# Split fp32r products for state and offset, and the pooling matrix folded into the output weights

## The reference, cut to what matters

```python
proj = rms_norm(h, norm_mix_w) @ w_in            # [u | z | xBC | dt]
y_pool = einsum(window_mean(u) - u, pool_w) * pool_scale       # 4 groups, windows 2, 4, 8, 16
x, B, C = silu(causal_conv4(xBC))                # 24 heads of 64 in 4 groups, state 128
# per chunk of 128 tokens and group of 6 heads:
y_diag = ((C B^T) * decay) @ (x * dt)
y_off  = exp(a_cs) * (C @ S)                     # S: the state carried from chunk to chunk
S      = S * chunk_decay + B^T @ (x * dt * decay_to_end)
y = (y_diag + y_off + d_skip * x) * silu(z)
y = y * rsqrt(mean(y * y) + eps) * ssm_norm_w    # mean over the 384 columns of the group
h = h + concat([y_pool, y]) @ w_out
h = h + relu(rms_norm(h, norm_ffn_w) @ w_ff1) ** 2 @ w_ff2
out = rms_norm(h, norm_f_w)[16:]
```

## Time and profile before

| | |
|---|---|
| median of 3 runs | 2752.06 us (2752.05 to 2752.53) |
| the profiled execution, its own time | 2754.46 us |
| its span | 2752.7 us |
| mean granted TensorE clock | 0.997 of full speed |
| TensorE busy | 2710.4 us, 98% of the span |
| VectorE, ScalarE, GpSimd busy | 58%, 45%, 40% |
| DMA | 531 MB, 193 GB/s in the mean |

### The profile page before, as it was taken

One profiled execution on the slowest core, in us unless ns is written; L12 is line 12 of the kernel. 1 busy time (PEld: TensorE's weight loads), 2 busy tenths in 40 slices (PEclk: granted clock), 3 DMA queues, 4 the chain that ended last, 5 costly groups with the idle time before them and its releaser, 6 DMA issues.

```text
span 2752.7 us, 37252 instructions
## 1 busy us (share of the span) xinstructions
PE 2710.4 (98%) x13950; PEld 2234.5 (81%) x13950; DVE 1609.6 (58%) x2221; ACT 1234.6 (45%) x2414; POOL 1093.3 (40%) x798
## 2 busy tenths in 40 slices
PE   8999999999999999999999999999999999999998
PEld 6778778888788887888888888878888888888887
DVE  3589833567425665147763466664445666666666
ACT  2367734556424555145552644555445322222323
POOL 1356641132101322003324587865655435353434
PEclk9999999999999999999999999999999999999999
DMA  9687576645556445565436546674444942333323
GB/s 291 206 272 235 198 273 246 240 161 197 182 200 260 157 148 204 198 233 208 167 144 244 189 157 224 238 265 166 154 141 167 350 153 92 138 122 131 122 92 153
DMA packets 225490, 531.12 MB, mean 193 GB/s; under 512 B 14090, under 2 KB 98062, under 8 KB 215838
## 3 DMA queue, kind: packets, MB, share of 16 engines
q1 hardware_dynamic: 225310, 528.74, 53.6%
HBM read 382.74 MB, written 145.95 MB: 192 GB/s over the span
## 4 chain that ended last, share of the span: by engine, by line
PE 92%; ACT 2%; DVE 2%; DMA 1%; issue 1%; POOL 1%; SPq 0%; DVEq 0%; ACTq 0%; POOLq 0%
PE bank L2007 22%; PE bank L1975 21%; PE bank L1697 19%; PE bank L1741 13%; PE bank L1721 6%; PE bank L1819 2%; PE bank L1812 2%; PE bank L1638 1%; PE bank L1793 1%; PE bank L1800 1%; PE bank L1776 1%; ACT E L1388 1%; DMA w_scr<-w_both 1%; PE bank L1760 1%; PE bank L1930 0%
## 5 line engine op out<-in xcount | busy, mean ns | idle before, releaser
L1697 PE MATMUL bank<-hnT_hi,w_ring 128*128 128x512 f32 x1152 | 374.4, 396 | 1.4 <-DMA w_ring<-w_scr 1.3
L2126 DVE SCALAR_TENSOR_TENSOR acc<-pre,par,acc 128x512 f32<-128x512 f32 x240 | 216.3, 901 | 108.7 <-ACT pre L1250 103.0
L2007 PE MATMUL bank<-w_first,T_hi 128*128 128x512 f32 x896 | 276.0, 389 | 0.3 <-issue 0.3
L1697 PEld LDWEIGHTS bank<-hnT_hi,w_ring 128*128 128x128 f32 x1152 | 216.5, 188 | 46.5 <-ACT pre L1250 1.4
L1975 PE MATMUL bank<-T_hi,w_both 128*128 128x512 f32 x768 | 242.6, 390 | 0.6 <-DMA T_lo<-hn_scr 0.4
L1741 PE MATMUL bank<-w_ring,T_hi 128*128 128x512 f32 x768 | 242.0, 396 | 0.0
L2449 DVE TENSOR_TENSOR acc_th<-bank,acc_th 128x512 f32<-128x512 f32 x224 | 149.9, 686 | 153.5 <-PE bank L2007 153.3
L1003 POOL TENSOR_TENSOR small<-small 128x1 f32<-128x1 f32 (+1 forms) x71 | 17.4, 245 | 546.2 <-ACT yo L1333 340.0
L1697 PE MATMUL bank<-hnT_lo,w_ring 128*128 128x512 f32 x576 | 224.8, 390 | 0.0
L1721 PE MATMUL bank<-w_ring,hnT_hi 128*128 128x384 f32 x768 | 198.4, 339 | 0.0
L2007 PEld LDWEIGHTS bank<-w_first,T_hi 128*128 128x128 f32 x896 | 168.1, 188 | 35.6 <-issue 0.7
(11 more groups left out here) (289 smaller groups left out, 6242.5 us busy)
## 6 DMA issues: line engine op xcount, KB each, us to landing
w_ring<-w_scr SPq DMA_DIRECT2D x312, 512.0 KB, 4.2
T_scr<-stage SPq DMA_DIRECT2D x32, 1792.0 KB, 6.8
w_scr<-w_both SPq DMA_DIRECT2D x104, 512.0 KB, 4.3
pair_raw<-in_w_ff SPq DMA_DIRECT2D x36, 1024.0 KB, 5.5
third<-T_scr SPq DMA_DIRECT2D x28, 1024.0 KB, 4.9
pair_raw<-T_scr SPq DMA_DIRECT2D x28, 1024.0 KB, 4.8
sums<-sums_scr SPq DMA_DIRECT2D x64, 384.0 KB, 4.9
raw<-in_w_in SPq DMA_DIRECT2D x36, 512.0 KB, 6.9
```

Of the source, the lines that this page charges most:

```text
L1697: mm = nc.tensor.matmul(bank[s][:, :], w[:, k, :], t[:, k, :], start=(k == 0 and j == 0), stop=(k == KT - 1 and j == 2))
L2007: mm = nc.tensor.matmul(bank[4 * half + t][:, :], a[:, k, tok], w[:, k, :], start=(SECOND[q % 7] not in GOES_ON and k == 0 and j == 0), st ...
L2126: ins = nc.vector.scalar_tensor_tensor(acc[:, s, 0:TB], pre[:, s, k:k + TB], w, acc[:, s, 0:TB], ALU.mult, ALU.add)
```

## The change

- The offset product C @ S and the state product B^T @ xw are done in three fp32r passes each instead of one fp32 matmul. The operands are split: ScalarE writes the high parts of C, S, xw and B (`c_both`, `s_both`, `xw_both`, `b_both`), GpSimd the low parts of C and S, VectorE those of xw and B. The buffers lie in the space of h, so h is loaded later, in the output projection.
- `slot3` is taken apart in `diagonal` and `state`. TensorE's order in a step is now: unit n1; `y_transposes` of q - 2; `diagonal` of q - 1; `slot1`; `state` of q - 1; unit n2; `y_offset`.
- The pooling matrix and scale are multiplied into the output weights once, in block 0 (`fold`: 8 products; four transposes of `pool_w` before), and so is the norm weight of y (`scale_rows`). The pooled values are split as they are.
- `y_high` and `y_low` are one instruction each; the history of the pooling windows is copied by ScalarE; S is scaled right after its low part is written; `state_add` comes before `taps`(n1).

```diff
@@ tensor
-                def y_offset(b, q, g, c):
-                    state_ready.wait(pe, b, q)
-                    nc.tensor.matmul(bank[7][:, 0:GW], group_tile(g, 1)[:, c * P:(c + 1) * P],
-                                     S[:, g, :], start=True, stop=True).then_inc(yoff_ps.sem, 1)
+                def y_offset(b, q):
+                    s_split_lo.wait(pe, b, q + 1)
+                    for j, (i, o) in enumerate(((0, 0), (0, 1), (1, 0))):
+                        mm = nc.tensor.matmul(bank[7][:, 0:GW], c_both[:, i, :], s_both[:, o, :],
+                                              start=(j == 0), stop=(j == 2))
+                    mm.then_inc(yoff_ps.sem, 1)
...
+                def state(b, q):
+                    xw_split_lo.wait(pe, b, q + 1)
                     yo_ready.wait(pe, b, q + 1)
-                    nc.tensor.matmul(bank[7][:, 0:GW], xb[:, GW:GW + P], xw[:, :],
-                                     start=True, stop=True).then_inc(state_ps.sem, 1)
+                    for j, (i, o) in enumerate(((0, 0), (0, 1), (1, 0))):
+                        mm = nc.tensor.matmul(bank[7][:, 0:GW], b_both[q % 2][:, i, :],
+                                              xw_both[:, o, :], start=(j == 0), stop=(j == 2))
+                    mm.then_inc(state_ps.sem, 1)
...
+                        if q > 1:
+                            y_transposes(b, q - 2)
                         if q:
-                            slot3(b, q - 1)
+                            diagonal(b, q - 1)
                         slot1(b, q, g, c)
+                        if q:
+                            state(b, q - 1)
                         for n in n2:
                             unit(b, n)
-                        y_offset(b, q, g, c)
-                        if q:
-                            y_transposes(b, q - 1)
...
+                    def fold(N):
...
+                        pe.wait_ge(raw_ready[N % RING], 16 * (N // RING + 1 + (N % RING == 0)))
+                        for kk in range(2):
+                            nc.tensor.matmul(bank[kk][:, :], pw[:, out_rows(N) + kk, :],
+                                             raw_half(N, kk), start=True, stop=True
+                                             ).then_inc(c_pe, 1)
...
-                                    nc.tensor.matmul(bank[2 + i % 2][:, :], pw[:, i, :],
-                                                     F[:, i * TB:(i + 1) * TB], start=True,
-                                                     stop=True).then_inc(mix_ps.sem, 1)
+                            if b == 0 and u in (1, 2):
+                                fold(N + 3)
@@ gpsimd, in a step behind ty = xb * d_skip
+                        s_split_hi.wait(pool, b, q + 1)
+                        nc.gpsimd.tensor_tensor(c_both[:, 1, :], group_tile(g, 1)[:, c * P:(c + 1) * P],
+                                                c_both[:, 0, :].bitcast(F32), ALU.subtract)
+                        nc.gpsimd.tensor_tensor(s_both[:, 1, :], S[:, g, :],
+                                                s_both[:, 0, :].bitcast(F32), ALU.subtract
+                                                ).then_inc(s_split_lo.sem, 1)
+                        gains_ready.wait(pool, b, 1)
+                        s_split_lo.wait(pool, b, q + 1)
+                        nc.gpsimd.tensor_tensor(by_head(S[:, g, :]), by_head(S[:, g, :]),
+                                                per_head(cd, c, g), ALU.mult
+                                                ).then_inc(scd_ready.sem, 1)
@@ scalar, in a step
+                        nc.scalar.activation(b_both[q % 2][:, 0, :], bank[4 + q % 2][:, GW:GW + P],
+                                             ACT.Copy)
+                        nc.scalar.activation(xb[:, :], bank[4 + q % 2][:, 0:GW], ACT.Copy
...
                         if q:
                             y_squares(b, q - 1)
+                        yoff_ps.wait(act, b, q)
+                        nc.scalar.activation(c_both[:, 0, :], group_tile(g, 1)[:, c * P:(c + 1) * P],
+                                             ACT.Copy)
+                        state_ready.wait(act, b, q)
+                        nc.scalar.activation(s_both[:, 0, :], S[:, g, :], ACT.Copy
+                                             ).then_inc(s_split_hi.sem, 1)
                         tanh(b, n1)
                         if q:
                             y_norm(b, q - 1)
+                        xw_ready.wait(act, b, q + 1)
+                        nc.scalar.activation(xw_both[:, 0, :], xw[:, :], ACT.Copy
+                                             ).then_inc(xw_split_hi.sem, 1)
@@ vector
+                def xw_low(b, q):
+                    xw_split_hi.wait(dve, b, q + 1)
+                    nc.vector.tensor_tensor(xw_both[:, 1, :], xw[:, :],
+                                            xw_both[:, 0, :].bitcast(F32), ALU.subtract
+                                            ).then_inc(xw_split_lo.sem, 1)
@@ sync
-                        if n == 12:
-                            sp.dma_start(h[:, :, :], x_in[0, b * TB:(b + 1) * TB, :].rearrange(
...
+                            if (d, i) == (0, 4):
+                                yoff_ps.wait(sp, b, STEPS)
+                                state_ps.wait(sp, b, STEPS)
+                                sp.dma_start(h[:, :, :], x_in[0, b * TB:(b + 1) * TB, :].rearrange(
```

More of the change, by code:

```diff
@@ L483, in weights_ready, with out_rows, raw_half, scale_rows @@
                 pe.wait_ge(w_loaded[(N - UNITS) % RING], 32 * ((N - UNITS) // RING + 1))
+        PW_SCALED = 7
+        PW_TURNED = 10
+        FOLDED = [U_OUT + d * 8 + u for d in range(2) for u in range(8) if OUT_ORDER[u] < 2]
+        def out_rows(N):
+            return 2 * OUT_ORDER[(N - U_OUT) % 8]
+        def raw_half(N, kk):
+            return raw[:, N % RING, kk * 512:(kk + 1) * 512]
+        def scale_rows(act, N):
+            if N in FOLDED:
+                f = FOLDED.index(N)
+                for kk in range(2):
+                    act.wait_ge(c_pe, PW_TURNED + 2 * f + kk + 1)
+                    last = nc.scalar.activation(raw_half(N, kk), bank[kk][:, :], ACT.Copy)
+            else:
+                for kk in range(2):
+                    w = W_NSSM + out_rows(N) + kk - 4
+                    last = nc.scalar.activation(raw_half(N, kk), raw_half(N, kk), ACT.Copy,
+                                                scale=par[:, w:w + 1])
+            last.then_inc(c_act, 1)
+            act.wait_ge(c_act, PW_SCALED + N - U_OUT + 1)
         def high_part(act, N):
@@ L1243, in evac @@
                         w3 = par[:, W_CONV + 60 + ct:W_CONV + 61 + ct]
-                        nc.scalar.activation(pre[:, s, 0:3], hist[:, ct, :], ACT.Copy
-                                             ).then_inc(hist_read.sem, 1)
+                        hist_read = steps.mark(nc.scalar.activation(
+                            pre[:, s, 0:3], hist[:, ct, :], ACT.Copy))
                         nc.scalar.activation(acc[:, s, 0:TB], ps, ACT.Identity, scale=w3,
                                              bias=par[:, W_BIAS + ct:W_BIAS + ct + 1])
-                        hist_read.wait(act, b, sum(conv_tile(m) is not None for m in range(n + 1)))
+                        steps.wait(hist_read)
                         nc.scalar.activation(hist[:, ct, :], ps[:, TB - 3:TB], ACT.Copy)
@@ L1316, in y_high @@
                         hT_stored.wait(act, b - 1, 16)
[L1317 to L1322, removed]
+                    nc.scalar.activation(T_hi[:, 4 + 3 * g:7 + 3 * g, c * P:(c + 1) * P],
+                                         bank[2][:, 0:GW].rearrange("p (i t) -> p i t", t=P),
+                                         ACT.Copy).then_inc(yT_hi.sem, 1)
                 def y_norm(b, q):
@@ L1358, in _ @@
                         evac(b, n)
+                        if b == 0 and n == 4:
+                            act.wait_ge(c_pe, PW_TURNED)
+                            for i in range(4):
+                                last = nc.scalar.activation(pw[:, i, :], bank[3][:, i * P:(i + 1) * P],
+                                                            ACT.Copy,
+                                                            scale=par[:, W_PSC + i:W_PSC + i + 1])
+                            last.then_inc(c_act, 1)
                         tanh(b, n - 1 if n else None)
@@ L1863, in _ @@
                                                  stop=True).then_inc(c_pe, 1)
+                        if b == 0 and n == 3:
+                            nv_ready.wait(pe, b, 1)
+                            for i in range(4):
+                                mm = nc.tensor.transpose(bank[3][:, i * P:(i + 1) * P], pw[:, i, :],
+                                                         ident[:, :])
+                            mm.then_inc(c_pe, 1)
                         if b and 1 <= n < 5:
```

132 lines of the change are left out of this document (71 added, 61 removed).

## The result

The changed kernel takes 2889.31 us (median of 4 runs, 2888.74 to 2894.04), the kernel before 2752.30 in the same comparison: a ratio of 1.0499, with an interval of 1.0486 to 1.0511. It is 137 us slower. The forecast was 2815 us, 63 slower, with a range up to 2850. So the direction was right and the size was not: the measured time lies outside the range.

A forecast was written before the change was run, and what follows sets the result against it. TensorE, busy 98% of the span, was taken to bound the kernel. Gains of 27 us against 86 of waits, 3 of other edits and 5 of VectorE interference gave +67, rounded to +63: 2815 us, range 2768 to 2850.

The forecast's parts named there:

- The waits at the offset product, 86 us: TensorE waits at the offset product for GpSimd's low part of S, 86 us over all blocks.
- The bounds of 60 to 125: Range in us given for the summed waits at the offset product, forecast at 86.
- the 1.4: Us added per step to ty's lateness at the offset product: low parts and semaphores less new cover; bounds 1.2 to 2.4.
- their 3.9 us of waits go: TensorE's waits at the transposes of y vanish because these move a step later, gaining 3.9 us.
- rival 1: TensorE's clock falls after the third-chunk waits, costing 12 to 24 us more, 2833 us; chance 0.16.
- 16.6 + 6.5: TensorE time gained: 16.6 us from three-pass offset and state products, 6.5 us net from folding the pooling products.
- -27 + 86 + 3 + 5: Sum in us: TensorE gains, offset-product waits, other edits in block 0, and VectorE slowing the low part of S.
- Rival 3: Each low part of S first waits out a VectorE instruction on the shared port: 25 us more, 2840 us; chance 0.10.
- Rivals 2 and 4: Chain ahead of the offset product hidden (2734 us, chance 0.11), or 1 us shorter than counted (2781 us, chance 0.13).
- cancel: Over the whole kernel gains and waits cancel, leaving 2752 us; chance 0.04.
- The 3 us allowed for other edits: Lateness in block 0 from half a microsecond more work per step on each engine, taken as 3 us.
- the 5 for VectorE beside the low parts: GpSimd's low part of S slowed by VectorE, 0.1 to 0.2 us in 34 steps, 5 us.

The follow-up runs named there:

- e1: Changed kernel with GpSimd's low parts of C and S ahead of its other work, and ScalarE's high parts before the sum of squares: 2827.51 us.
- e6: e3 with the transposes of y moved behind the state product: 2748.18 us, 0.9983 of the kernel before.
- e3: Changed kernel with the offset product as one fp32 matmul again, without any split of C and S: 2787.64 us.
- e8: Offset product in fp32, state product split, transposes of y back in their old place behind the offset product, against e3: 2743.31 us.
- e9: e8 with the state product of block 0 in fp32 too: 2739.21 us, 0.9949 of the kernel before.
- e7: Changed kernel with both products in fp32 and TensorE's old order, keeping the folding and small edits: 2745.17 us, 0.9971 of the kernel before.
- e5: Changed kernel with the moves of e1 and e2 together: 2797.37 us, 1.0165 of the kernel before.
- e2: Changed kernel with the transposes of y behind the state product instead of ahead of the diagonal products: 2869.74 us.

## Why the prediction was wrong

- **The waits at the offset product, 86 us: right.** 78.8 came, at the place and by the releaser named. By kind of step in blocks 1 to 3, the first chunks wait 1.35 to 1.37 us (0.55 forecast), the second 1.45 to 2.10 (1.9), the third 2.66 to 2.76 (3.2), the fourth nothing, and eight of the twelve single steps 0.52 to 0.55 (0.6 to 0.7). Block 0 has 25.6 us (29), its first step 6.2 of them (5.3). Single terms were off and cancelled: the low part of C lasts 0.65 us (0.4 taken) and that of S 1.26 in the mean (1.02 taken), while `ty` in the third chunk lasts 0.83 (1.38 in the earlier trace rows) and so comes earlier. That the order on GpSimd and ScalarE decides was shown by e1, the two not apart. The bounds of 60 to 125 don't follow from the working: it had the 1.4 at no less than 1.2 and no more than 2.4, and over its some 52 steps that is 76 to 138; 78.8 lies in both.
- **The step that failed: "their 3.9 us of waits go".** I put the moved transposes at a gain because y was a step older, and looked only at their input. The bank that they write is freed by `y_low`, on VectorE behind `yo`, which needs the offset product just issued. The forecast had 3.9 us going to nothing and they went to 47.2, so the term is wrong by 47 us, most of the 72 by which the forecast missed the span. The runs show it alone: moving the transposes further back gains 39.4 us (e6 against e3), and returning them to their old place 44 (e8 against e3). What I should have asked of a moved instruction is not only whether its operand is ready, but what frees its output.
- **The clock, rival 1: right in kind and in place, but not all of it.** The sum put it at nothing and the rival at a chance of 0.16 and 12 to 24 us. It came beside the forecast and not in its place: the clock's loss rose by 38 us. Windows of the kernel after, behind the third-chunk wait shown above (us, busy PE PEld DVE ACT POOL, PEclk, DMA share, GB/s):

```profile
1113.00:1114.00 1.00, 1.00 (x6) 1.00 (x7) 1.00 (x2) 0.51 (x2) 0.95 (x1) 1.00 0.00 0
1114.00:1115.00 1.00, 1.00 (x6) 1.00 (x5) 1.00 (x2) 0.74 (x2) 0.14 (x1) 0.64 0.00 0
1115.00:1116.00 1.00, 1.00 (x5) 1.00 (x4) 1.00 (x3) 0.00 (x0) 0.29 (x1) 0.50 0.00 0
1116.00:1117.00 1.00, 1.00 (x5) 1.00 (x4) 0.09 (x1) 0.00 (x0) 0.72 (x1) 0.50 0.00 0
1117.00:1118.00 1.00, 1.00 (x6) 1.00 (x5) 0.00 (x0) 0.00 (x0) 0.00 (x0) 0.66 0.06 16
1118.00:1119.00 1.00, 1.00 (x7) 1.00 (x6) 0.00 (x0) 0.00 (x0) 0.00 (x0) 1.00 0.00 0
```

  TensorE works from 1112.96 at full clock, and between 1114 and 1115 the grant falls to 1.2 GHz in the midst of matmuls, for some 3 us. My bound "the waits may come out under 3" did not hold: 2.66 was enough here. For the nine third chunks the rival's price was about right: seven of their waits are followed by such a fall, which costs some 1.7 us each (0.36 + 0.50 + 0.50 + 0.34 in the rows above), 12 us together. The rest, two thirds of the 38, I had not counted: most of it lies in block 0 (0.93 over 270 us, 0.98 before) and in the single steps, where the new waits at the transposes stand. e3, without the offset waits, has 17 us of clock loss, and e9, almost without waits, 5.5.
- **TensorE's gains: the 23 us of passes (16.6 + 6.5) held where TensorE did not wait.** Folding 6.5 held (7.5 in e7, with the small edits). The state product went from 0.74 to 0.62, 0.12 of the 0.13 forecast. The offset product has two costs. Where it starts straight behind the unit in front, it takes 0.52, the forecast's 3 x 0.174: six rows of the kernel after and 29 of e1, 0.52 to 0.54. Where it starts late, even by 0.14 us, it takes 0.62 to 0.65: 34 of the 38 other rows of the kernel after from which the cost can be read (the last four are longer still). So the first passes behind a stop cost 0.11 more, some 5 us in all for the 47 waits (an estimate), which belong to the price of a wait and not to that of the split. Why it is so is not settled.
- **Sum.** -27 + 86 + 3 + 5 gave 67. With what the rows show: 79 (offset) + 47 (transposes) + 38 (clock) - 18 (passes: the 23.1 forecast less the 5 behind the stops) = 146, against 134.6 in the span. The busy part of it fits (38 - 18 = 20, measured 20.3). Of the idle part the old 3.9 us at the transposes are to be taken off, and the rest of TensorE's idle fell from 42.3 - 3.9 = 38.4 to 156.6 - 126.0 = 30.6 us: small waits that the new ones swallowed, of which I had guessed half in the rounding from 67 to 63. That leaves 134. The 3 us allowed for other edits and the 5 for VectorE beside the low parts are not seen as terms of their own.
- **Rival 3 (shared port, 25 us)** was a part of the truth: low parts of S last 0.99 to 1.44 us, 1.26 in the mean, and not 1.02 plus 0.55; the lock bites in block 0 instead, at `xw_low`. Rivals 2 and 4 and "cancel" are excluded by the waits.

Not settled: why one wait of 2.7 us is followed by a fall of the clock and another of the same length is not (those that end at 726.46 and 1497.96, 2.66 and 2.71 us, keep 1.00 in every microsecond of the five behind them); whether the low parts of C and S would be hidden on VectorE (not tried); and whether block 0 of e5 can be ordered so that all splits fit. What the offset split could win, if its low parts were hidden, is 64 x (0.65 - 0.52) = 8.3 us; that is an estimate, and no run reached it.

## What to carry to other kernels

When an instruction is moved ahead of others on the engine that bounds the kernel, trace both ends: what makes its input, and what frees its output, each back through the program order of the engines that do it, to see if one of them waits for something that the bounding engine does only just before. Put the producers of the bounding engine's operands first in the queues of the helpers, and take a split of an operand only if its rows fit in the slack ahead of the consumer, which here was 0.85 us for 2 us of work to save at most 0.13. Repair all waits that stand in series before judging one repair, since the next wait takes part of the gain: in e2, 37 us of waits went at the transposes and 20 came up at the offset product.

## What the runs showed of the hardware

- A granted clock that falls after TensorE has resumed: idle 2.66 us, full clock for at least 1 us, then 0.64 and 0.50. Over the whole kernel a microsecond of the new waits cost about 1.3 us, an estimate from 126 us of waits and 38 us of clock loss; single waits in the third chunks brought none or some 1.7 us.
- VectorE's 384-column `xw_low` takes 0.55 us alone and 2.69 us beside a GpSimd instruction of 1024 columns that lasts 2.78.
- Three fp32r passes of 384 columns between two units cost 0.52 us from start to start, as 3 x 0.174 from a long row gives, when TensorE comes to them without a stop, and 0.62 to 0.65 when it had stopped, even for 0.14 us.
- Filler matmuls in front of a wait gave back 7.4 us, though they add work: the granted clock of block 2's ordinary steps rose from 0.96 to 1.00.
